# Loading the low halves of the queries once, and scoring them over 64 rows, in a two-branch attention and MoE block

## The reference

```python
h = rmsnorm(x, norm_mix)
qa, ka, va, qb, kb, vb = split(h @ w_in)
ya = swa_gqa_sinks(rope(qa), rope(ka), va, attn_sinks) @ w_o_a    # own chunk of 64 and one before; 8 q heads, 2 kv heads
yb = chunk_relbias_attention(qb, kb, vb, rel_bias) @ w_o_b        # own chunk and 8 before; 8 heads, bias by distance
gates = sigmoid(h @ w_branch_gate + b_branch_gate)
x = x + (gates[0] * ya + gates[1] * yb) @ w_out
x = x + hierarchical_moe(rmsnorm(x, norm_ffn), ...)               # top 1 of 4 groups, top 2 of 8 experts in it
out = rmsnorm(x, norm_final)
```

## Time and profile before

| | us |
|---|---|
| median of three runs | 2852.53 |
| lowest and highest | 2847.73, 2854.17 |
| the profiled execution | 2847.73 |
| its span, first to last instruction | 2846.0 |
| PE busy, PE weight loads busy | 2376.4, 2017.5 |
| DVE, ACT, POOL busy | 1334.1, 1049.8, 699.2 |
| mean granted clock of PE | 0.926 |

### The profile page before, as it was taken

One profiled execution on the slowest core, in us unless ns is written; L12 is line 12 of the kernel. 1 busy time (PEld: TensorE's weight loads), 2 busy tenths in 40 slices (PEclk: granted clock), 3 DMA queues, 4 the chain that ended last, 5 costly groups with the idle time before them and its releaser, 6 DMA issues. The chain is left out here.

```text
span 2846.0 us, 37025 instructions
## 1 busy us (share of the span) xinstructions
PE 2376.4 (83%) x12254; PEld 2017.5 (71%) x12255; DVE 1334.1 (47%) x1962; ACT 1049.8 (37%) x1705; POOL 699.2 (25%) x693
## 2 busy tenths in 40 slices
PE   3899996899996888655599999829999999999940
PEld 2788875688885777555488888828888888888830
DVE  7101221100001777545433223267766767787958
ACT  4211111111112777534311111125644646666722
POOL 4254555520000000000212122012322323333432
PEclk9999998999997999878799899959999999999975
DMA  4245557671215555286544343257866868888958
GB/s 141 79 143 163 184 192 185 192 302 72 82 59 157 143 143 143 53 192 172 180 141 133 110 130 115 94 195 263 316 238 231 320 229 320 299 342 324 375 227 328
DMA packets 238591, 548.57 MB, mean 193 GB/s; under 512 B 56032, under 2 KB 90272, under 8 KB 232496
## 3 DMA queue, kind: packets, MB, share of 16 engines
q1 hardware_dynamic: 191120, 409.12, 43.7%
q0 software_dynamic: 27056, 89.67, 9.4%
q10 hardware_dynamic: 20336, 48.77, 4.7%
HBM read 413.46 MB, written 134.02 MB: 192 GB/s over the span
## 5 line engine op out<-in xcount | busy, mean ns | idle before, releaser
L394 DVE TENSOR_TENSOR pj_w_lo<-pj_w_raw,pj_w_hi 128x1024 fp32r<-128x1024 f32 x46 | 61.5, 1339 | 665.9 <-ACT pj_w_hi L333 665.7
L333 ACT ACTIVATE pj_w_hi<-pj_w_raw 128x1024 fp32r<-128x1024 f32 x46 | 48.6, 1059 | 640.7 <-PE pj_bank L436 525.2
L436 PE MATMUL pj_bank<-pj_hT_hi,pj_w_hi 128*128 128x512 f32 x960 | 257.6, 390 | 3.5 <-DVE pj_w_lo L394 3.5
L436 PE MATMUL pj_bank<-pj_hT_lo,pj_w_hi 128*128 128x512 f32 x960 | 257.4, 390 | 0.0
L436 PE MATMUL pj_bank<-pj_hT_hi,pj_w_lo 128*128 128x512 f32 x960 | 257.3, 390 | 0.0
L1768 POOL TENSOR_TENSOR ex_wd_lo<-weights_raw_d,ex_wd_hi 128x1024 fp32r<-128x1024 f32 x64 | 194.4, 3059 | 131.7 <-ACT ex_wd_hi L1793 131.7
L436 PEld LDWEIGHTS pj_bank<-pj_hT_hi,pj_w_hi 128*128 128x128 f32 x960 | 180.8, 188 | 41.3 <-DVE pj_w_lo L394 3.9
L436 PEld LDWEIGHTS pj_bank<-pj_hT_hi,pj_w_lo 128*128 128x128 f32 x960 | 180.8, 188 | 37.6
L436 PEld LDWEIGHTS pj_bank<-pj_hT_lo,pj_w_hi 128*128 128x128 f32 x960 | 180.8, 188 | 37.6
L1415 PE MATMUL mg_y_ps<-mg_aT_hi,mg_w_hi 128*128 128x256 f32 x512 | 155.3, 303 | 57.1 <-DVE mg_aT_lo L1327 49.3
L1858 DVE TENSOR_TENSOR ex_wd_lo<-weights_raw_d,ex_wd_hi 128x1024 fp32r<-128x1024 f32 x64 | 169.1, 2681 | 9.8 <-ACT ex_wd_hi L1793 9.8
(11 more groups left out here) (245 smaller groups left out, 5654.1 us busy)
## 6 DMA issues: line engine op xcount, KB each, us to landing
weights_raw_g<-in_w_exp_gate_dram SPq DMA_DIRECT2D x128, 512.0 KB, 6.0
weights_raw_u<-in_w_exp_up_dram SPq DMA_DIRECT2D x128, 512.0 KB, 6.5
weights_raw_d<-in_w_exp_down_dram SPq DMA_DIRECT2D x128, 512.0 KB, 6.1
scratch_ys<-ex_y ACTq DMA_DIRECT2D x47, 512.0 KB, 4.4
pj_w_raw<-in_w_feat_dram SPq DMA_DIRECT2D x46, 512.0 KB, 6.0
scratch_gates<-pj_f_hi SPq DMA_DIRECT2D x32, 512.0 KB, 3.4
scratch_ys<-pj_g_row POOLq DMA_DIRECT2D x32, 512.0 KB, 16.3
mg_g_in<-scratch_gates SPq DMA_DIRECT2D x128, 128.0 KB, 2.9
```

The lines of the kernel that those rows point to most:

```text
L333: act.activation(w_hi[n % 2][:], w_raw[n % 2][:], ACT.Copy).then_inc(whi_done, 1)
L394: dve.tensor_tensor(w_lo[n % 2][:], w_raw[n % 2][:], w_hi[n % 2][:], ALU.subtract).then_inc(wlo_done, 1)
L436: last = pe.matmul(eight[4 * p + b][:], w[p][:, k * P:(k + 1) * P], h[:, k, b * NB:(b + 1) * NB], start=(k == 0 and n == 0), stop=(k == KD ...
```

## The change

The q_lo matmul runs over the 64 partitions of k hi alone: the product q_lo·k_lo is left out, so `q_lo` needs one copy, in partitions 0 to 63, and one load in place of two. This is done in both attentions. In `attend_b` a head has five loads in place of six (512 KB less), in `attend_a` a segment three in place of four (1 MB less). The matmuls of q_hi and the number of all matmuls stay.

```diff
-        q_lo = [st.sb(f"q_lo{p}", [P, SEQ], F32R) for p in range(2)]
+        q_lo = [st.sb(f"q_lo{p}", [DH, SEQ], F32R) for p in range(2)]
...
-        QK_LOADS = 6
+        QK_LOADS = 5
...
-                for part, turned in enumerate((q_hi, q_lo)):
-                    for half in range(2):
-                        sp.dma_start(turned[p][half * DH:(half + 1) * DH, :].bitcast(F32), qk[part, q, rows, :]
-                                     ).then_inc(qk_in[p], 16)
+                for half in range(2):
+                    sp.dma_start(q_hi[p][half * DH:(half + 1) * DH, :].bitcast(F32), qk[0, q, rows, :]).then_inc(qk_in[p], 16)
+                sp.dma_start(q_lo[p][:].bitcast(F32), qk[1, q, rows, :]).then_inc(qk_in[p], 16)
...
-                    last = pe.matmul(s_ps[:, c:c + w], q_lo[hd % 2][:, tok], k_st[hd % 2][:, keys], start=False, stop=True)
+                    last = pe.matmul(s_ps[:, c:c + w], q_lo[hd % 2][:, tok], k_st[hd % 2][:DH, keys],
+                                     start=False, stop=True)
...
-        q_lo = [st.sb(f"q_lo{p}", [P, WINDOWS // 2, Q_HEADS * CHUNK], F32R) for p in range(2)]
+        q_lo = [st.sb(f"q_lo{p}", [DH, WINDOWS // 2, Q_HEADS * CHUNK], F32R) for p in range(2)]
...
-        Q_LOADS = 4
+        Q_LOADS = 3
...
-                for turned, part in ((q_hi, hi), (q_lo, lo)):
-                    for half in range(2):
-                        sp.dma_start(turned[seg % 2][half * DH:(half + 1) * DH, :, :].bitcast(F32), part
-                                     ).then_inc(q_in[seg % 2], 16)
+                for half in range(2):
+                    sp.dma_start(q_hi[seg % 2][half * DH:(half + 1) * DH, :, :].bitcast(F32), hi).then_inc(q_in[seg % 2], 16)
+                sp.dma_start(q_lo[seg % 2][:].bitcast(F32), lo).then_inc(q_in[seg % 2], 16)
...
-                    last = pe.matmul(out, q_lo[seg % 2][:, here, rows], k_st[g][:, keys], start=False, stop=True)
+                    last = pe.matmul(out, q_lo[seg % 2][:, here, rows], k_st[g][:DH, keys], start=False, stop=True)
```

## The result

| | before | after |
|---|---|---|
| median, us | 2851.8 | 2926.89 |
| span of the profiled execution | 2846.0 | 2917.1 |
| ratio of the times, 95% interval | | 1.0238 [1.0211, 1.0265] |

A forecast was written before the change was run, and what follows sets the result against it. Chunked attention: PE, DVE and ACT nearly balanced; sliding-window attention: transfers bound its start. Loads -2.3, chunked attention +19, sliding-window attention +9.4 sum to +26 us, forecast 2878 us; own range 2855 to 2917, stated range 2835 to 2905.

The forecast's parts named there:

- Loads: Fewer loads: first scores 2.3 us sooner in chunked attention, 4.9 in sliding-window attention, whose waits for v and late q go.
- the first rival: Both attentions: only the loads count, PE's work is unchanged; 17.4 us faster, 2835 us; chance 0.16.
- The price of a boundary: Switches between 128-row and 64-row instructions on PE: 0.15 us extra each, 0.18 ahead of a 512-column matmul, at full clock.
- the 0.10 in which the array was to empty: Part of each row-count switch on PE: about 0.10 us for the array to drain, beside unhidden load and matmul.
- The slack: Chunked attention: PE's waits for row maximum and issue, 56.7 us in 128 units, about 0.44 us a unit.
- I let all of it be used: Chunked attention: PE's whole 56.7 us of slack absorbs added work, so 75 - 57 = +18 us.
- +19 for stage b: Chunked attention: +18 us of PE work beyond its slack, +1 for units in which DVE also collects.
- half the slack, +47: Chunked attention, upper bound: only half of PE's slack is usable, giving +47 us.
- a rival, for stage a throughout: Sliding-window attention wholly at 1.2 GHz because PE is thinly used: 58 us more, 2936 us; chance 0.04.
- 4 us of clock as won in stage a: Sliding-window attention: with two waits gone, less work at half clock after them, about 2 us back for each.
- the 1 us of the start: Chunked attention: 1 us of PE time added for the half clock at its start, beside 74 us for boundaries.
- -2.3 + 6 + 1: Low end of the forecast's own range: loads -2.3, chunked attention +6, sliding-window attention +1, given as 2855 us.

The follow-up runs named there:

- e3: Changed kernel's loads, but q_lo matmul over all 128 rows with the lower half of q_lo zeroed once; 0.9938 of the kernel before, median 2833.06 us.
- e6: Changed kernel with the q_hi matmuls also over 64 rows, so all scores over 64 rows; 1.0267 of the kernel before.
- e8: Kernel before plus, in the chunked attention, a 4-column matmul over 128 rows ahead of each score pair; 1.0055 of the kernel before.
- e9: Kernel before with sliding-window attention as in e3, plus a 4-column matmul over 64 rows ahead of each q_hi matmul there; 1.0257 of the kernel before.
- e5: Changed kernel with q_lo first in each second score pair, so half the boundaries; 1.0114 of the kernel before.
- its control: Same as e9 but the 4-column matmuls run over 128 rows, so no boundary; 0.9963 of the kernel before.
- e7: Kernel before plus, in the chunked attention, a 4-column matmul over 64 rows ahead of each score pair; 1.0136 of the kernel before.

## Why the prediction was wrong, point by point

**Loads: right.** Stage b's first scores came at 902.17 with the stage 0.95 us early, so 2.4 us sooner (2.3 said). Stage a's came 4.7 us sooner after its start (4.9 said), the waits for v and the late q went. e3 measured the sum: 18 us by the ratio, against the first rival's 17.4. By stage its profile shows 1.3 (2.3 said) and 13.7 (15.1 said).

**The price of a boundary: right at full clock.** 0.43 and 0.26 us against 0.42 and 0.26, a step of 3.14 against 3.18. It came from a handful of boundaries around another instruction, and the 0.10 in which the array was to empty is still a guess: the runs measure the sum, not its parts. At half clock I had 0.23; it is 0.19 behind a 128-column matmul (0.40 where 0.21) and 0.30 to 0.33 behind a 512-column one. The Trainium skill's rule that a change of the tiling mode drains TensorE (TensorEngine Tiling, Key Properties) agrees with these rows. The Trainium skill's other rule, that loads overlap matmuls only in other row groups (TensorE: Matmul & The Clock Gate, Part 3, The mechanism), does not: in e6 loads of 64 rows follow matmuls of the same 64 after 0.11 and 0.23 us, as hidden as over 128 rows.

**The slack: wrong by 13 us.** The step that failed is "I let all of it be used". The sum had +19 for stage b; at full clock the units grew by 0.25 us, 32 us. PE added 0.59 us a unit (75 / 128) and 0.34 of it were hidden, not 0.44. e8 shows this without any boundary: of 0.19 us added, 0.09 showed. The slack of three engines that wait for each other in turn is not a reserve that is used up first. The bound that I gave (half the slack, +47) held the stage's 32 at full clock.

**The clock: the larger miss, some 27 us in stage b and 8 to 10 in stage a.** I priced the lower clock only as a rival, for stage a throughout, with a chance of 0.04, on the ground that the clock rose there under load. What failed is that argument: the load had been that of 128-row matmuls without gaps. And I had counted 4 us of clock as won in stage a. PE had 23 us more at 1.2 GHz there than before (47 against 11, 10 and 3), four to five steps of 5.25 us in place of 3.14, or 9. e6 and e9 had the rival's case in full, and e5 for most of the stage. For stage b the clock stood only in the 1 us of the start; that it could fall there didn't occur to me.

Forecast 26 us; with 13 for the slack and 27 and 8 for the clock the sum is 74, less the 3.7 that the other stages gave, 70, against the 71 of the span. That it closes so well is partly arithmetic: in stage b the counts of units times their lengths make up the stage by construction, and the 8 is what was left over in stage a. The lower end of the forecast's own range has a slip too: -2.3 + 6 + 1 on 2852.5 is 2857, not 2855.

**What stays open.** That gaps hold the clock down in stage a is shown by e9 and its control. For stage b it is shown that gaps alone bring no dips (e7), and that more 64-row work at an unchanged number of boundaries does (e6 against e5). It is not shown that the rows alone do it: e6 still has two boundaries a unit. Nor is it shown why gaps alone brought no dips in stage b, where the clock had risen once: stage a differs in its columns, its step and in starting behind a longer pause, and these were not varied one at a time. All lengths of low stretches are of one execution each.

## What to carry to other kernels

Halving the rows of a matmul saved no TensorE time here, and between neighbours of another row count it cost 0.15 to 0.19 us each time at full clock. If fewer rows are wanted to save a copy of data, keep the full height and put zeros there once: e3 was faster than the kernel before. Grouping the matmuls of one height halved the gaps and still left the kernel 1.1% slower than before (e5). Slack read from waits hid about half of what was added to this loop of balanced engines (0.10 of 0.19 us in e8, 0.34 of 0.59 in the change), so put the middle into the sum, not the best. And a change that makes TensorE's work thinner, by gaps or by rows, has to be priced at both clocks: look for the granted clock of each stretch, not only at the instruction's cost.

## What the runs showed that I had not expected

At 1.2 GHz a boundary costs more: a load behind a 512-column matmul comes after 0.73 to 0.76 us in place of 0.43, at 2.4 GHz after 0.43 in place of 0.24. The clock followed the rows: with all scores over 64 rows, at an unchanged distance of the loads within a unit (0.11 and 0.23 us), 44.2 us went by at 0.50 from the first scores of stage b. The same start took 11.1 us in the kernel before, 17.1 in e5, 18.6 in e7 and 27.6 in the changed kernel. And the clock followed the gaps where it stood low already: 189 us at 0.50 in e9, 16.7 in its control.
